# TensorE takes 37 instead of 25 of the first half's expert dots, and the second half's top-k moves into the first half's part

## The reference

```python
q = (xt @ w_query).reshape(T, PEER_HEADS, PEER_KEY_DIM)
s1 = jnp.einsum('thd,hkd->thk', q[..., :PEER_HALF], sub_keys_1)
s2 = jnp.einsum('thd,hkd->thk', q[..., PEER_HALF:], sub_keys_2)
v1, i1 = lax.top_k(s1, PEER_TOPK)           # 16 of 128 keys, twice
v2, i2 = lax.top_k(s2, PEER_TOPK)
cand = v1[..., :, None] + v2[..., None, :]  # 256 sums a head
top_s, pos = lax.top_k(cand, PEER_TOPK)     # 16 experts a head
g = jax.nn.softmax(top_s, axis=-1)
# for each token, over its 8 heads x 16 experts:
a = jax.nn.gelu(jnp.einsum('cd,ced->ce', xi, expert_down[ei]))
out = jnp.einsum('ce,ced->cd', a * gi, expert_up[ei])
```

## Time and profile before

| | us |
|---|---|
| median of 3 runs (lowest, highest) | 2147.24 (2146.65, 2147.27) |
| the profiled execution | 2147.69 |
| span of its records | 2145.9 |
| PE busy | 1848.2 (86%) |
| DVE busy | 1565.7 (73%) |
| ACT busy | 875.9 (41%) |
| POOL busy | 800.1 (37%) |

### The profile page before, as it was taken

One profiled execution on the slowest core, in us unless ns is written; L12 is line 12 of the kernel. 1 busy time (PEld: TensorE's weight loads), 2 busy tenths in 40 slices (PEclk: granted clock), 3 DMA queues, 4 the chain that ended last, 5 costly groups with the idle time before them and its releaser, 6 DMA issues.

```text
span 2145.9 us, 27518 instructions
## 1 busy us (share of the span) xinstructions
PE 1848.2 (86%) x11035; PEld 1624.1 (76%) x11035; DVE 1565.7 (73%) x1874; ACT 875.9 (41%) x1235; POOL 800.1 (37%) x490
## 2 busy tenths in 40 slices
PE   9989999999999999588871234399999999999997
PEld 7859976999999889577771133278888888888886
DVE  5424435444356468799999999866788888999998
ACT  4323334434333443122220579774434444433443
POOL 0302200000000000676665667412454444677882
PEclk9989996999999999799995555599999999999999
DMA  7475540355557544899999889727999999999996
GB/s 256 159 242 191 175 157 1 104 189 177 179 190 260 195 147 162 365 426 426 426 426 396 348 337 423 291 73 288 365 375 427 393 387 386 364 403 408 392 391 257
DMA packets 142664, 620.04 MB, mean 289 GB/s; under 512 B 9681, under 2 KB 20193, under 8 KB 84465
## 3 DMA queue, kind: packets, MB, share of 16 engines
q0 software_dynamic: 46352, 336.11, 38.8%
q1 hardware_dynamic: 93712, 280.05, 35.9%
q10 hardware_dynamic: 2512, 2.75, 0.4%
HBM read 616.77 MB, written 2.10 MB: 288 GB/s over the span
## 4 chain that ended last, share of the span: by engine, by line
PE 68%; DVE 16%; ACT 5%; DMA 5%; POOL 3%; issue 3%; DVEq 0%; ACTq 0%
PE psum L608 67%; DVE down_rows L2003 10%; DMA down_rows<-in_peer_expert_down_dram,eidx 3%; ACT oh L1513 1%; POOL down_rows L1139 1%; POOL c_lo L1166 1%; POOL late_rows L1139 1%; ACT W L1534 1%; ACT oh L1521 1%; ACT W L1526 1%; DMA pe_rows<-in_peer_expert_down_dram,eidx 1%; DMA u_raw<-in_peer_expert_up_dram 1%; DVE w_lo L1665 1%; DMA raw<-in_w_in_dram 1%; PE psum L825 0%
## 5 line engine op out<-in xcount | busy, mean ns | idle before, releaser
L1139 POOL DMA_INDIRECT down_rows<-in_peer_expert_down_dram,eidx x171 | 323.0, 1889 | 753.6 <-DVE w_lo L1665 597.6
L1665 DVE TENSOR_TENSOR w_lo<-raw,w_hi 128x2048 fp32r<-128x2048 f32 x124 | 285.6, 2303 | 365.4 <-ACT w_hi L1230 365.3
L1230 ACT CAST w_hi<-raw 128x2048 fp32r<-128x2048 f32 x124 | 236.1, 1904 | 435.5 <-PE psum L608 406.7
L608 PE MATMUL psum<-u_hi,c_hi 128*128 128x512 f32 x1024 | 400.1, 391 | 5.5 <-POOL c_lo L1166 4.6
L608 PE MATMUL psum<-u_hi,c_lo 128*128 128x512 f32 x1024 | 399.2, 390 | 0.0
L608 PE MATMUL psum<-u_lo,c_hi 128*128 128x512 f32 x1024 | 399.1, 390 | 0.0
L2003 DVE CUSTOM_DVE_ANT_0 down_rows<-down_rows,xn 128x2048 f32<-128x2048 f32 x171 | 385.3, 2288 | 12.5 <-DMA down_rows<-in_peer_expert_down_dram,eidx 11.0
L2108 DVE TENSOR_TENSOR u_lo<-u_raw,u_hi 128x2048 fp32r<-128x2048 f32 x128 | 303.6, 2371 | 100.0 <-ACT u_hi L1569 98.5
L608 PE MATMUL psum<-act_hi,w_hi 128*128 128x256 f32 x1088 | 310.7, 286 | 8.7 <-DVE w_lo L1665 8.7
L608 PE MATMUL psum<-act_lo,w_hi 128*128 128x256 f32 x1088 | 309.2, 284 | 0.0
L608 PE MATMUL psum<-act_hi,w_lo 128*128 128x256 f32 x1088 | 309.2, 284 | 0.0
(11 more groups left out here) (300 smaller groups left out, 2878.6 us busy)
## 6 DMA issues: line engine op xcount, KB each, us to landing
u_raw<-in_peer_expert_up_dram SPq DMA_DIRECT2D x128, 1024.0 KB, 7.5
raw<-in_w_in_dram SPq DMA_DIRECT2D x76, 1024.0 KB, 5.0
raw<-in_w_out_dram SPq DMA_DIRECT2D x16, 1024.0 KB, 5.0
raw<-in_peer_w_query_dram SPq DMA_DIRECT2D x16, 1024.0 KB, 4.9
raw<-in_w_up_nsa_dram SPq DMA_DIRECT2D x8, 1024.0 KB, 5.0
raw<-in_w_up_fox_dram SPq DMA_DIRECT2D x8, 1024.0 KB, 5.0
raw<-in_k_cmp_w_dram SPq DMA_DIRECT2D x4, 1024.0 KB, 5.4
raw<-in_v_cmp_w_dram SPq DMA_DIRECT2D x4, 1024.0 KB, 8.3
```

Source lines behind the costliest of these rows:

```text
L608: return nc.tensor.matmul(*a, skip_group_check=True, **k)
L1139: nc.gpsimd.indirect_dma_start(rows[:], None, table, bass.IndirectOffsetOnAxis(ap=eidx[:, half, slot:slot + 1], axis=0)).then_inc(landed, 16)
L1230: nc.scalar.copy(w_hi[:, p % 2], raw[:, p]).then_inc(hi_done, 1)
L1665: tt(w_lo[:, p % 2], raw[:, p], f32(w_hi[:, p % 2]), ALU.subtract).then_inc(lo_done, 1)
```

## The change

`PE_SLOTS` is now every third slot from 9 to 117, 37 in all, with four `pe_rows` buffers; so DVE has 91 instead of 103 of the first half's dots and 37 instead of 25 short `diag_dot`. The useless matmuls behind a PE dot go from 6 to 2. The 18 top-k parts of pairs 2 to 7 are spread over G 2 to G 15 by a table: part j stands behind G 2 + j*14//18, so that G 2, 5, 9 and 12 have two parts and the other ten one; none is left in the second part. `topk_weights` of a pair now stands two groups behind its end. ACT's exponentials follow. Both halves share one one-hot scratch tile (`onehot`). PE makes the second half's key scores ahead of slot 45 (57 before) and the transposed indices ahead of slot 57 (73).

```diff
--- before.py
+++ after.py
@@ -131,13 +131,15 @@
 NG = (DENSE[0] + DENSE[1]) // GS
 SPREAD_G = SLOTS // GS
 NUM1_AT = 16
-PE_SLOTS = tuple(range(9, 106, 4))
+PE_SLOTS = tuple(range(9, 118, 3))
 DIAG_BEHIND = 7
-PE_RING = 3
+PE_RING = 4
 ROUNDS = 4
-WARM = 6
-SCORES_1_AT = 57
-NUM0_AT = 73
+WARM = 2
+SCORES_1_AT = 45
+NUM0_AT = 57
+TOPK_PARTS = {(1, 1): 0, (1, 2): 1}
+TOPK_PARTS.update({(2 + j // 3, j % 3): 2 + j * 14 // 18 for j in range(18)})
 DVE_ROWS = 1
 LATE_AT = (10, 74, 18, 82, 0)
 LATE_FREE = (16, 16, 32, 32, 0)
@@ -243,7 +245,7 @@
 
 
         down_rows = [at(f"down_rows{r}", [P, D], 42 + 8 * r if r < 4 else 8 * r - 22) for r in range(RING)]
-        onehot = [at(f"onehot{half}", [P, PEER_H, TOPK, TOPK], kb) for half, kb in enumerate((114, 178))]
+        onehot = at("onehot", [P, 2, TOPK, TOPK], 195)
         cand = at("cand", [P, 2, TOPK, TOPK], 154)
         cand2 = at("cand2", [P, 2, TOPK * TOPK], 156)
         list2 = at("list2", [P, 4, NKEYS], 158)
@@ -259,7 +261,7 @@
 
         rT = at("rT", [P, ROUNDS, 4, P], 74)
         xT = at("xT", [P, KC, P], 82)
-        pe_rows = [at(f"pe_rows{r}", [P, D], kb) for r, kb in enumerate((90, 98, 130))]
+        pe_rows = [at(f"pe_rows{r}", [P, D], kb) for r, kb in enumerate((90, 98, 130, 122))]
         diag = at("diag", [P, P], 194)
         numT = at("numT", [P, HALVES, 2, P], 0.5)
         dots = at("dots", [P, HALVES, SLOTS], 2.5)
@@ -1546,7 +1548,7 @@
             soft_pairs([0])
             for r in range(4):
                 row_out(r)
-            soft_at = {1: 1, 2: 4, 3: 7, 4: 10, 5: 13}
+            soft_at = {k: TOPK_PARTS[k, 2] for k in range(1, 8)}
             for n_, t in enumerate(PE_SLOTS):
                 for k in [k for k in soft_at if GS * soft_at[k] + GS <= t]:
                     soft_pairs([k])
@@ -1575,10 +1577,6 @@
                 spread_out(b)
                 if b + 2 < NB:
                     one_hots_0(b + 2)
-                if b == 1:
-                    soft_pairs([6])
-                if b == NUM1_AT - 4:
-                    soft_pairs([7])
                 if b == NUM1_AT:
                     numbers_out_pairs()
                 if b == NB - 6:
@@ -1950,7 +1948,7 @@
                 settle()
                 full = [P, nh, TOPK, TOPK]
                 iota = const("iota").unsqueeze(1).to_broadcast([P, ns, TOPK])
-                eq = onehot[half][:, hs]
+                eq = onehot[:]
                 oh = eq.rearrange("p h s c -> p (h s) c")
                 ks = slice(h0 * TOPK, h1 * TOPK)
                 for l in range(2):
@@ -2167,22 +2165,22 @@
 
             def between(G):
 
-
-                if G < 2:
-                    k, part = 1, G + 1
-                else:
-                    k, part = ((G - 2) // 3 + 2, (G - 2) % 3) if G < 8 else ((G - 8) // 3 + 4, (G - 8) % 3)
-                half, h = k // 4, 2 * (k % 4)
-                if part == 0:
-                    topk_weights(k, (k - 1) // 4, 2 * ((k - 1) % 4), 2 * ((k - 1) % 4) + 2)
-                    dve.wait_ge(ks_ps, 4 if half == 0 else 5)
-                    top_lists(half, h)
-                    top_lists(half, h + 1)
-                elif part == 1:
-                    top_sums(half, h)
-                    top_sums(half, h + 1)
-                else:
-                    topk_end(half, h, h + 2)
+                for (k, part), at_ in TOPK_PARTS.items():
+                    if at_ + 2 == G and part == 2 and k < 7:
+                        topk_weights(k + 1, k // 4, 2 * (k % 4), 2 * (k % 4) + 2)
+                for (k, part), at_ in TOPK_PARTS.items():
+                    if at_ != G:
+                        continue
+                    half, h = k // 4, 2 * (k % 4)
+                    if part == 0:
+                        dve.wait_ge(ks_ps, 4 if half == 0 else 5)
+                        top_lists(half, h)
+                        top_lists(half, h + 1)
+                    elif part == 1:
+                        top_sums(half, h)
+                        top_sums(half, h + 1)
+                    else:
+                        topk_end(half, h, h + 2)
 
             for G in range(NG):
                 for q in range(4 if G == 0 else 0, GS):
@@ -2198,8 +2196,7 @@
                         t, n_ = GS * (G - SPREAD_G) + q - 2, GS * (NG - SPREAD_G) - 8
                         for b in range(min(NB, NB * max(t, 0) // n_), min(NB, NB * max(t + 1, 0) // n_)):
                             one_hots_0(b)
-                if G < SPREAD_G + 4:
-                    between(G)
+                between(G)
                 if G == SLOTS // GS - 1:
                     weights(0)
                 if G == NG - 4:
```

## The result

| | before | changed |
|---|---|---|
| median (lowest, highest), us | 2147.26 (2146.65, 2150.38), 4 runs | 2128.31 (2125.25, 2129.47), 4 runs |
| ratio, 95% interval | | 0.9907 [0.9889, 0.9924] |
| the profiled execution, us | 2147.69 | 2125.25 |
| span of its records, us | 2145.9 | 2123.4 |

The changed kernel is 18.95 us (0.9%) faster by the medians. The forecast was 2131.4 us. The profiled execution of the changed kernel is its fastest run, 3.1 us under its median, so the two traces differ by 22.5 us: more than the change is worth.

The account below looks back on a forecast made before the run. The prediction took DVE, with the gathers also full, to bound the first part and ACT the second; 2147.69 + 1.2 - 17.0 = 2131.9 us for the profiled execution, 2131.4 us for the median, range 2125 to 2141 us.

Parts of the forecast that it names:

- The second part: From the first half's weights to the second half's: ACT bounds it and loses its top-k waits, 17.0 us shorter.
- The case in which all 23.5 us count: Rival, second part: ACT is not the bound, all 23.5 us taken off DVE are won, 2125 us; chance 0.05.
- The first part: Slot 23's dot to the first half's weights: moved top-k and diag_dots refill DVE's saved dots, 1.2 us longer.
- its start is the same: Slot 23's dot, where the first part starts, still waits for its row's gather and ends as before.
- Costs nothing: First part: POOL's later PE gathers cost 0 while the DMA queue is not empty, with a lead of 9 to 10 slots.
- PE late: Rival, first part: PE dots over 7.8 us delay DVE; chances 0.07 up to 10 us, 0.05 for 11 to 20, 0.05 more.
- four long waits of PE for a `diag_dot`: First part, while DVE makes two top-k parts in a row: slower PE clock might cost 8 us in all, taken as 0.
- The gathers in the second part: Rival: gathers and loads after 1196 us decide only under 371 GB/s; at 335, 2150 us; chance 0.03.
- SP's loads would cost nothing: Second part: three expert_up loads ahead of the gathers of rows 136 on cost 0, at most 7.4 us less DVE's spare.
- The marks: Expected profile times: first half's weights at 1196 to 1198 us, the second half's near 1377 us.
- The expected small waits of DVE for PE: Second part: DVE shows small waits for PE at its one-hot rows and is busy about 86%.

Follow-up runs that it names:

- e4: The changed kernel with DVE making two of each block's four first one-hot rows instead of one: 2119.97 us, ratio 0.9875.
- e8: The changed kernel with five instead of four buffers for PE's rows: 2127.08 us, ratio 0.9913.
- e5: The changed kernel with three instead of four buffers for PE's rows: 2147.55 us, ratio 0.9999.
- e3: The changed kernel with 6 instead of 2 useless matmuls behind each PE dot: 2139.40 us, ratio 0.9969.
- e6: The changed kernel with 0 instead of 2 useless matmuls behind each PE dot: 2128.83 us, ratio 0.9917.
- e2: The changed kernel with the 25 PE dots, three buffers for PE's rows and 6 useless matmuls of before, top-k still moved: 2151.23 us, ratio 1.0023.

## Why the prediction was right, and where it was off

**The second part** was the larger term, and it held: 17.0 us forecast, 17.1 measured (197.2 to 180.1); all seven profiles with the new top-k order and one row of DVE's a block give 180.0 or 180.1. ACT's waits of the earlier trace rows went and nothing took their place, at 4.96 us a block as forecast. That ACT was the bound, and hence 6.5 of DVE's 23.5 us would be lost, is shown by e4: with one row a block less for ACT, the part lost another 7.9 us. The case in which all 23.5 us count is out.

**The first part** was a term of +1.2 us and measured -0.5. The kinds and counts of instructions were right; the durations were a little high. Over the whole part, the 72 dots and 34 diag_dots take 166.6 us (166.9 forecast), the 18 top-k parts 105.5 us (107.1 forecast), and DVE waits 0.5 us. A dot repeats at 919.29 - 917.08 = 2.21 us, not 2.22. A `topk_end` behind `topk_weights` takes 948.62 - 943.22 = 5.40 us, not 5.60; the one at the end of the part takes 1191.91 - 1186.20 = 5.71. The price of the lists, 6.60 us, had a wait of 0.19 us in it, which its own row shows in brackets. The parts vary by a few tenths of a microsecond, and I took each price from a single row. The mean of all its repetitions would have been the better price. The sum is right in its main point: what DVE is spared in dots the moved top-k fills.

**The start.** The step "its start is the same" is neither shown nor refuted. Slot 23's dot ended 3.3 us earlier in the first profile and 1.9 us earlier in the second, and in the other kernels between 2.8 us earlier and 0.8 us later than before, in no order that the edits explain. From slot 4's dot to slot 23's end it is 50.2 us before, 50.2 and 50.0 after; so it is when the first rows arrive that varies.

**Gathers and rooms.** "Costs nothing" was right for four rooms, and e8 confirms it. But the reason given (a lead of 9 to 10 slots in place of 10.7) does not say how near the edge four rooms are. Counted the same way for e5, a lead of 6 to 7 slots, it gave a loss of 2 to 10 us where 19.5 were measured. What the count left out is POOL's order: a room of PE's rows that comes free late stops the gathers of both kinds, here for up to 13.8 us, and DVE then waits for rows for which it had rooms.

**PE late** did not happen: the clock was 0.97 in the window where I asked for over 0.9, a PE dot 6.70 us against 6.66 counted. I feared four long waits of PE for a `diag_dot`; there are seven waits (24.5 us in all), six of them over 2 us, and behind five of these the clock was at its lower level. Still DVE waited for no PE dot. The point from which this rival decides was wrong: not 7.8 us a dot but somewhere between 6.70 and 7.60 (e3). The spare was thinner than the forecast said: by the 6.9 us for three slots of a fast group (under e3) it was 0.2 us a dot there, not 0.7 to 1.1. That the term came out at 0 was in part luck. It was the cut from 6 useless matmuls to 2 that kept it: with the rest of the change in place it is worth 10.5 us, more than half of the gain.

**The gathers in the second part** moved 427 GB/s from 1196 to 1291 us at a share of 1.01, where only under 371 would have decided; now with SP's three loads among them. The 358 of the Trainium skill ("DMA: Bandwidth & Descriptors", in "Where 436 GB/s comes from") is passed here again. The 335 GB/s of the earlier trace rows were therefore no limit of the transfers. That SP's loads would cost nothing held too: in the second part DVE waited for no row.

**The marks.** Expected: first half's weights at 1196 to 1198 us, measured 1191.91 and 1193.37. By my own rule ("if at 1190 or under, my count of DVE's work is wrong") the count stands; the earlier mark is 1.7 us of durations and the rest the start. Expected weights of the second half near 1377 us, measured 1372.01 and 1373.36, the same difference carried on. The expected small waits of DVE for PE at L2089 are there, 17 such waits, 12.3 us in all (6.9 us in 10 before):

```profile
DVE oh L2089 <- PE psum L610: 12.3, 17, 2.4
```

DVE's busy share in the part is 165.0 of 180.1 us, 92%, not 86%. I had taken the ratio within a block (4.2 of 4.96 us) for that of the whole part, at whose ends DVE has dots and no block to wait for.

**The median.** -0.5 and -17.1 make 2147.3 - 17.6 = 2129.7 us; measured were 2128.31, 2128.94, and 2127.08 for e8. The 1 to 3 us that are left lie in the start, the second half's spread (37.9 to 39.3 us over all profiles) and the up phase (712.1 to 715.3 us). These stages differ between executions without an edit in them, and their cause stays open.

## What to carry to other kernels

When an engine can't work ahead by more than two steps, price its deadline by the fastest stretch that it must follow, not by the mean. Two edits that each win little or lose alone (here 6.2 us won and 4.2 us lost) may win 18 together, if one frees time on the engine that the other fills while a second resource (here the DMA) is already full. When a wait on an issuing queue is long, look at the share of what it feeds before you call it harmless or a cause; and once an engine is found to be the bound, moving one small item of it to the engine behind is the next gain (7.9 us here for one row a block).

## What the runs showed of the hardware

- Indirect gathers of 8 KB rows ran at 425 or 426 GB/s and a DMA share of 1.01 on one core, from 931 to 1127 us, in eight of the twelve profiles (421 in e6; at a lower share 407 in e3, 410 in e2 and 386 in e5), and with SP's loads at 427 GB/s from 1196 to 1291 us in the changed kernel.
- The issue of a gather on POOL takes 0.94 us in many rows and up to 3.1 us in others of the same form, and the difference goes with DVE's dots. In the traces before and after, from 900 to 1190 us, every one of the 137 issues that start while a dot runs ends 3.09 to 3.11 us after the start of that dot, however late in the dot it started; of the 91 others, 71 take 0.93 to 0.95 us. The POOL rows shown under e5 follow it: the issues at 942.52 (1.77 us) and 944.60 (1.91 us) end at 944.29 and 946.51 us, 3.09 and 3.10 us after the starts of these two dots, and the one at 946.81 us, with no dot running, takes 0.94 us.

```profile
941.20 2.29 DVE L2001 CUSTOM_DVE_ANT_0 down_rows<-down_rows,xn 128x2048 f32<-128x2048 f32 x1
943.41 2.29 DVE L2001 CUSTOM_DVE_ANT_0 down_rows<-down_rows,xn 128x2048 f32<-128x2048 f32 x1
```

- PE's clock is lower behind some of its waits: in the changed kernel eight products take 1.95 us behind an idle time of 2.29 us, at a granted clock of 0.53 (the lower level, 1.2 GHz), where others take 1.13 us. It is back at 998.36 us, 3.9 us later (1.00 from 998.4 to 1001 us). Not every wait does this: behind one of 2.50 us, at 1074.65 us, eight products took 1.13 us at a granted clock of 1.00.

```profile
994.43 1.95 PE L610 MATMUL psum<-xT,rT 128*128 128x128 f32 x8 [2.29 <-DVE dots L2018]
996.17 1.06 PE L942 MATMUL psum<-ct,pe_rows 128*128 128x128 f32 x4
997.02 1.50 PE L610 MATMUL psum<-xT,rT 128*128 128x128 f32 x8
998.36 0.60 PE L942 MATMUL psum<-ct,pe_rows 128*128 128x128 f32 x4
```

The transposes of four take 1.06 us and then 0.60 us. Without any useless matmuls (e6) the granted clock from 931 to 1127 us was still 0.95.
